# Retention's heads overlapped and stick-breaking cut to 512 queries, with its dense groups reordered

## What is computed

```python
proj = hn @ w_in
rq, rk, rv, rg, sq, sk, sv, ga, gb = split(proj)
q_r = rotary(heads(rq, 4)) * 256 ** -0.5        # 4 heads of 256, values of 512
k_r = rotary(heads(rk, 4))
y_ret = head_groupnorm(retention(q_r, k_r, heads(rv, 4)))   # decay g_h ** (t - s), causal
y_ret = (silu(rg) * y_ret) @ w_ret_out
y_sb = stick_breaking(heads(sq, 16), heads(sk, 16), heads(sv, 16)) @ w_sb_out
merged = sigmoid(ga) * y_ret + sigmoid(gb) * y_sb
mix = merged @ w_out
```

## Time and profile before

| | us |
|---|---|
| median of 3 runs (3181.03 to 3189.07) | 3181.04 |
| the profiled execution | 3180.37 |
| its span in the trace | 3178.6 |
| TensorE busy over the span (94%) | 2988.1 |
| VectorE (DVE) busy (46%) | 1473.8 |
| ScalarE (ACT) busy (34%) | 1082.3 |

### The profile page before, as it was taken

One profiled execution on the slowest core, in us unless ns is written; L12 is line 12 of the kernel. 1 busy time (PEld: TensorE's weight loads), 2 busy tenths in 40 slices (PEclk: granted clock), 3 DMA queues, 4 the chain that ended last, 5 costly groups with the idle time before them and its releaser, 6 DMA issues.

```text
span 3178.6 us, 47047 instructions
## 1 busy us (share of the span) xinstructions
PE 2988.1 (94%) x18149; PEld 2585.7 (81%) x18149; DVE 1473.8 (46%) x2073; ACT 1082.3 (34%) x1706; POOL 203.3 (6%) x169
## 2 busy tenths in 40 slices
PE   8999999999999766999999898998999999899997
PEld 7887789999999666899987786776888887678885
DVE  5554445553344666555543443344433334544423
ACT  4334333332333333343322222132334443333221
POOL 1000010000100232100001101001000000200000
PEclk9999999999999877999999999999999999899998
DMA  4221123233333000133333132131311112233331
GB/s 120 57 60 50 50 60 92 86 91 86 118 93 86 26 0 0 53 93 92 91 89 108 53 93 62 57 95 34 96 51 40 48 45 63 70 93 93 91 97 57
DMA packets 419421, 225.50 MB, mean 71 GB/s; under 512 B 7461, under 2 KB 416294, under 8 KB 419222
## 3 DMA queue, kind: packets, MB, share of 16 engines
q1 hardware_dynamic: 416310, 211.45, 23.2%
q0 software_dynamic: 2256, 10.32, 1.0%
q10 hardware_dynamic: 784, 2.75, 0.2%
HBM read 222.36 MB, written 2.13 MB: 71 GB/s over the span
## 4 chain that ended last, share of the span: by engine, by line
PE 83%; issue 10%; DVE 4%; ACT 2%; POOL 1%; DMA 0%; DVEq 0%; POOLq 0%; ACTq 0%
PE ps L425 36%; PE ps L421 28%; PE ps L630 3%; PE ps L712 2%; PE ps L804 2%; PE ps L914 2%; PE ps L900 1%; PE ps L714 1%; PE ps L871 1%; PE ps L724 1%; PE ps L634 1%; PE ps L817 1%; PE ps L903 1%; PE ps L695 1%; DVE g_qk L1700 0%
## 5 line engine op out<-in xcount | busy, mean ns | idle before, releaser
L393 DVE TENSOR_TENSOR wl<-raw,wh 128x1024 fp32r<-128x1024 f32 (+2 forms) x421 | 511.6, 1215 | 430.7 <-ACT wh L389 428.7
L389 ACT ACTIVATE wh<-raw 128x1024 fp32r<-128x1024 f32 (+2 forms) x421 | 425.8, 1011 | 802.2 <-PE ps L421 426.4
L425 PE MATMUL ps<-xh,wh 128*128 128x264 f32 x2736 | 565.2, 288 | 7.8 <-DVE xl L454 6.0
L425 PE MATMUL ps<-xl,wh 128*128 128x264 f32 x2736 | 559.0, 286 | 0.0
L425 PE MATMUL ps<-xh,wl 128*128 128x264 f32 x2736 | 558.5, 286 | 0.0
L425 PEld LDWEIGHTS ps<-xh,wh 128*128 128x128 f32 x2736 | 428.6, 189 | 14.5 <-issue 3.9
L425 PEld LDWEIGHTS ps<-xl,wh 128*128 128x128 f32 x2736 | 426.0, 189 | 0.0
L425 PEld LDWEIGHTS ps<-xh,wl 128*128 128x128 f32 x2736 | 425.2, 189 | 0.0
L421 PE MATMUL ps<-xh,wh 128*128 128x512 f32 x976 | 393.6, 403 | 17.9 <-DVE xl L454 14.0
L421 PE MATMUL ps<-xl,wh 128*128 128x512 f32 x976 | 389.0, 399 | 0.0
L421 PE MATMUL ps<-xh,wl 128*128 128x512 f32 x976 | 386.8, 396 | 0.0
(11 more groups left out here) (292 smaller groups left out, 4051.2 us busy)
## 6 DMA issues: line engine op xcount, KB each, us to landing
raw<-in_w_in SPq DMA_DIRECT2D x88, 512.0 KB, 4.0
raw<-in_ffn_w_gate SPq DMA_DIRECT2D x44, 512.0 KB, 3.8
raw<-in_ffn_w_up SPq DMA_DIRECT2D x44, 512.0 KB, 3.8
raw<-in_w_ffn_in SPq DMA_DIRECT2D x44, 512.0 KB, 3.8
raw<-in_fox_w_in SPq DMA_DIRECT2D x33, 512.0 KB, 4.1
raw<-in_hgrn_w_in SPq DMA_DIRECT2D x32, 512.0 KB, 4.0
raw<-in_ffn_w_down SPq DMA_DIRECT2D x32, 448.0 KB, 3.7
raw<-in_ffn_w_down SPq DMA_DIRECT2D x16, 512.0 KB, 3.9
```

Of the source, the lines that this page charges most:

```text
L389: nc.scalar.activation(wh[:, v % 2, 0:nk, :], raw[:, v % RAW_SLOTS, 0:nk, :], ACT.Copy).then_inc(s("w_hi"), 1)
L393: nc.vector.tensor_tensor(wl[:, v % 2, 0:nk, :], raw[:, v % RAW_SLOTS, 0:nk, :], wh[:, v % 2, 0:nk, :].bitcast(F32), ALU.subtract).then_in ...
L425: last = nc.tensor.matmul(ps[:, bank + b, 0:HALF], w[:, slot, kk, :], x[:, k, b * HALF:(b + 1) * HALF], start=first, stop=end_)
```

## The change

**Retention.** The heads are pipelined. A prologue `PH_RETP` makes q0, q1, k0, k1, v0, v1 of head 0 and its scores and decay. A pass of `PH_RET` (three) then makes `RET_REST` of its own head (v2, v3, g0 to g3), `RET_NEXT` of the next (q0, q1, k0, k1, v0, v1) and its own output projection; the last head (`PH_RETL`) makes the five `ga` groups where the others have `RET_NEXT`. Groups are as many in sum, and as many narrow and wide. TensorE's pass (where lines are left out stand the transposes and the values' matmuls, unchanged):

```diff
+            for gj in range(3):
+                group(gj)
+            pe.wait_ge(s("psum_free"), evacuated(PH_RETL, 0, 1) if last_ else evacuated(PH_RET, i, 1))
             pe.wait_ge(s("r_s_ready"), i + 2)
...
+            last.then_inc(s("r_vt_mm"), 1)
+            group(3)
+            pe.wait_ge(s("r_vt_ready"), 2 * i + 1)
...
+            group(4)
             pe.wait_ge(s("r_vt_ready"), 2 * i + 2)
...
+            group(5)
+            group(6)
             mean(0, "r_mu_mm")
+            group(7)
+            group(8)
             mean(1, "r_var_mm")
+            for gj in range(9, n_out):
+                group(gj)
             for m in range(KT):
+                group(n_out + m, ("r_out_ready", 4 * i) if m == 0 else None)
+                if m == 3 and not last_:
+                    ret_scores(i + 1)
```

On DVE the order of a pass becomes:

```diff
+            for uj in range(7):
+                split(uj)
+                take(uj)
             dve.wait_ge(s("r_mu_mm"), i + 1)
...
+            split(7)
+            take(7)
+            if not last:
+                dve.wait_ge(s("psum_free"), evacuated(ph, n, 7))
+                rotate(i + 1, 0)
+            split(8)
+            take(8)
             dve.wait_ge(s("r_r"), i + 1)
+            dve.wait_ge(s("r_g"), 4 * i + 4)
...
+                if e == 1:
+                    split(9)
+                    take(9)
+            split(10)
...
+            take(10)
+            if not last:
+                dve.wait_ge(s("psum_free"), evacuated(ph, n, 9))
+                rotate(i + 1, 1)
+                split(11)
+                take(11)
...
+                if m == 4 and not last:
+                    decayed(i + 1)
```

**Stick-breaking, 512 queries.** The strips become retention's (`QSTRIP`, 512, 400, 272, 144 and 16 columns), for the real tokens only:

```diff
-            for j in (0, 1, 3, 2):
-                nc.tensor.matmul(flat[:, STRIP0[j]:STRIP0[j] + SEQ - P * j], s_k[lo:hi, P * j:P * j + P],
-                                 s_q[lo:hi, P * j:SEQ], start=(j != 3), stop=False, skip_group_check=True)
             for j in range(NTT):
-                nc.tensor.matmul(flat[:, tail_at(j):tail_at(j) + TAIL], s_k[lo:hi, P * j:P * j + P],
-                                 s_q[lo:hi, SEQ:L], start=False, stop=False, skip_group_check=True)
+                nc.tensor.matmul(flat[:, QSTRIP[j]:QSTRIP[j] + SEQ - QFIRST[j]], s_k[lo:hi, P * j:P * j + P],
+                                 s_q[lo:hi, QFIRST[j]:SEQ], start=(j < 3), stop=False, skip_group_check=True)
```

**Stick-breaking, order.** The groups become values, gate, queries, keys; the transposes of the values (`sb_turn`) move from ahead of the sums to behind the last group:

```diff
+            ahead_(0)
             if not isinstance(i, int) or i:
                 sb_values(i - 1, 1)
+            sb_sums(2 * i)
+            ahead_(1)
+            pe.wait_ge(s("sb_a"), 2 * i + 1)
+            sb_z(1)
+            ahead_(2)
+            pe.wait_ge(s("sb_vt_ready"), i + 1)
+            pe.wait_ge(s("sb_o_done"), i + 1)
+            sb_values(i, 0)
+            sb_sums(2 * i + 1)
+            ahead_(3)
+            if not last:
+                pe.wait_ge(s("psum_free"), evacuated(PH_SB, i, 0))
+                sb_turn()
+                pe.wait_ge(s("psum_free"), evacuated(PH_SB, i, 3))
+                pe.wait_ge(s("sb_a"), 2 * i + 2)
+                sb_z(0)
```

More of the change, by code:

```diff
@@ L276, in program @@
     a = Area(after_yr, end)
+    b = Area(norms_at, arena)
+    ident_r, later_r, tri_r, one_r = (b.take(f"{n}_r", [P, P], F32R) for n in ("ident", "later", "tri", "one"))
+    assert b.at <= norms_at + 4 * L
     gb = a.take("gb", [P, KT, L])
@@ L840, in _, with ret_scores @@
         feed_forward(1, PH_UP1, PH_DOWN1, 3, 3)
[L843 to L857, removed]
+        def ret_scores(i):
             pe.wait_ge(s("r_rot"), i + 1)
@@ L1230, in _, with ret, high @@
         residual(PH_DOWN1, 4, ROW_MIXPRE)
-        def ret(i, norm=None):
+        for uj in range(N_NEXT):
+            split_ahead(act, act_hi, PH_RETP, 0, uj)
+            if uj == 0:
+                act_rstd(act, 4)
+        def ret(i, last=False):
+            ph, n = (PH_RETL, 0) if last else (PH_RET, i)
             def split(uj):
-                split_ahead(act, act_hi, PH_RET, i, uj)
+                split_ahead(act, act_hi, ph, n, uj)
             def gate(uj):
-                act.wait_ge(s("psum_free"), evacuated(PH_RET, i, uj))
-                nc.scalar.activation(rt[:, uj, META:L], rt[:, uj, META:L], ACT.Silu).then_inc(s("r_g"), 1)
-            for uj in range(8):
-                split(uj)
-                if norm and uj == 0:
-                    norm()
+                act.wait_ge(s("psum_free"), evacuated(ph, n, uj))
+                t = rt[:, RET_ROW["g"] + uj - 2, META:L]
+                nc.scalar.activation(t, t, ACT.Silu).then_inc(s("r_g"), 1)
+            def high(e):
+                act.wait_ge(s("r_out"), 4 * i + e + 1)
+                copy(rh[:, e, META:L], r_y[:, e, :]).then_inc(s("r_out_hi"), 1)
+            tables_for(act, "silu")
+            split(0)
+            split(1)
+            split(2)
+            gate(2)
             act.wait_ge(s("r_vt_mm"), 2 * i + 1)
             copy(r_vt[:, 0:NFULL, :], ps[:, 4:8, :]).then_inc(s("r_vt_ready"), 1)
+            split(3)
+            gate(3)
             act.wait_ge(s("r_vt_mm"), 2 * i + 2)
             copy(r_vt[0:TAIL, NFULL, :], ps[0:TAIL, 7, :]).then_inc(s("r_vt_ready"), 1)
-            split(8)
+            split(4)
+            gate(4)
+            split(5)
             act.wait_ge(s("r_y_mm"), i + 1)
             copy(r_y[:, :, :], ps[:, 4:8, :]).then_inc(s("r_y_ready"), 1)
-            split(9)
-            gate(8)
+            split(6)
+            gate(5)
+            tables_for(act, "ln_exp")
+            split(7)
             for e in range(4):
```

313 lines of the change are left out of this document (165 added, 148 removed).

## The result

| | before | after |
|---|---|---|
| median of the runs, us | 3181.03 (3179.16 to 3189.07, 4 runs) | 3085.14 (3083.71 to 3086.73, 4 runs) |
| profiled execution, us | 3180.37 | 3086.73 |
| its span, us | 3178.6 | 3085.0 |

The ratio is 0.9694, interval [0.9676, 0.9712]: faster by 95.9 us, to 3085.14 us where 3091 (3077 to 3114) was predicted.

The account below looks back on a forecast made before the run. TensorE was taken to bound both stages, by gaps in retention, matmul count and price in stick-breaking, and half clock. 59.8 + 17.9 - 3.5 + 15.7 = 89.9 us off 3180.37 gave 3091 us, range 3077 to 3114.

Parts of the forecast that it names:

- Retention: 59.8 us predicted: Retention stage: 45.5 us of TensorE waits and 19.6 us of half clock go, less 5.3 us coming back.
- what was to come back (5.3 us): Retention: 3.3 us of new TensorE waits on DVE, plus 2 us for more changes between dense groups and small matmuls.
- just in time: Retention, DVE: take 7, first rotation and split 8 end at 12.2 us, as group 8 ends; no wait.
- Stick-breaking, work: Stick-breaking matmuls: cheaper `z` and values, sums slightly dearer, sixteen times; 17.9 us saved, bounds 12 and 20.
- Order: 3.5 us predicted: Stick-breaking: keys come last, so the next pair's `z` waits for their eviction; 0.5 us seven times lost, bounds 2.5 and 7.
- Clock: 15.7 us predicted: Stick-breaking: half-clock stretches follow `z` with its tails; 3 of 18.7 us stay, 15.7 go, bounds 0 and 18.7.
- The dense groups on both sides of `z(1)`: Stick-breaking: with these and the tails gone, `z(1)` was expected to lower the clock no more.
- The first, that the half clock stays: Stick-breaking rival: stretches occur without idle time, so removing idle time can't cure them; 3107 us, chance 0.20.
- seven drops: Stick-breaking: if transposes don't count as busy, a drop of 1.7 us stays at each `z(0)`; 3100 us in all.
- The second rival: Retention: DVE becomes the bound of groups 9 to 11, 5 us a head; 3111 us, chance 0.12.
- The third: Retention rival: the chain still ends bare at the output projection, 6.67 + 2.4 us a head return; 3127 us, chance 0.04.
- the slower one: Retention rival: the whole chain lies bare on DVE, 39 us a head at most; 3247 us, chance 0.02.

Follow-up runs that it names:

- e8: Changed kernel with three thrown-away DVE multiplies added ahead of each head's first rotation; 3103.2 us in its one run.
- e4: Changed kernel with DVE's split 11, for out tile 0, put ahead of the second rotation; 3081.52 us, ratio 0.9688.
- e9: Kernel before with only the 512 queries in stick-breaking, nothing else changed; 3144.89 us, ratio 0.9884.
- e2: Changed kernel with the old stick-breaking order of groups (values, queries, keys, gate) and transposes, 512 queries kept; 3081.02 us, ratio 0.9687.
- e3: Changed kernel with the new order kept but 528 queries and the 16-column tails put back; 3121.09 us, ratio 0.9812.
- e5: Changed kernel with five thrown-away 16-column matmuls added to each `z`; 3120.02 us, ratio 0.9792.
- e6: Changed kernel with three thrown-away matmuls of 256, 256 and 128 columns added to each `z`; 3105.88 us, ratio 0.9748.
- e10: The changed kernel itself, unaltered, measured again in a second study; 3087.79 us, ratio 0.9705.
- e1: Changed kernel with all of stick-breaking put back (528 queries, strips, order), retention kept; 3125.69 us, ratio 0.982.
- e7: Changed kernel with old stick-breaking order, split 11 ahead of the second rotation, decay multiplies one output tile later, last head's ACT split ahead of the fifth sigmoid; 3073.84 us.

## Why the prediction was right

**Retention: 59.8 us predicted, 64.1 measured.** All 45.5 us of waits and all the half clock went, as the text had it: nothing but the stretch at the entry of the stage is left. Of what was to come back (5.3 us), the listed waits on `wl` come to 3.3 us, the sum that was forecast, but their places are not those of the forecast, and the agreement of the sum is luck. The timeline of DVE in head 1:

```profile
1939.82 0.69 DVE L1517 TENSOR_TENSOR rt<-ps,rstd 128x512 f32<-128x512 f32 x1 [0.99 <-PE ps L425]
...
1945.06 1.22 DVE L397 TENSOR_TENSOR wl<-raw,wh 128x1024 fp32r<-128x1024 f32 x1
...
1959.30 0.70 DVE L1517 TENSOR_TENSOR rt<-ps,rstd 128x528 f32<-128x528 f32 x1
1963.99 0.69 DVE L397 TENSOR_TENSOR wl<-raw,wh 128x512 fp32r<-128x512 f32 x1 [0.15 <-DVE rt L1802]
...
1984.79 1.73 DVE L1811 TENSOR_TENSOR r_s<-ps,decay 128x512 f32<-128x512 f32 x4
```

- The first rotation stands between take 7 and split 8, which ends at 1946.28; group 9, which needs it, began at 1946.33. The forecast put this split "just in time", with no cost, and 0.2 us on split 9, which cost nothing (it ended at 1951.90, ahead of group 9's end). In fact TensorE did wait for split 8: group 9 starts 0.86 us behind the variance, where behind the mean, and behind both in the last head, which has no rotation, it is 0.46. That is 0.40 us in each of three heads, 1.2 us, which no listing shows, since the modelled end of the variance covers it. e8 confirms it: all of the 3.75 us more came through.
- Behind the second rotation the split of the first half group (split 11) came at 1963.99, and TensorE waited 0.63 us, forecast 0.7. e4 took this wait away.
- A third, of 0.24 us at output tile 6, was not foreseen: the decay multiplies of the next head (1984.79) stand ahead of that split on DVE. The last head waited 0.65 us, not 0.4.
- The 4.3 us by which the step was short: idle time fell by 43.6 us, which is 45.5 and the 1.3 us of waits on `r_sum` that the forecast left out, less 3.3. The 2 us set aside for more changes between dense groups and small matmuls don't show as such. Busy time fell by 20.5 us, where 19.6 was worked out and 19.1 is half of what was busy at half clock; the other 1.4 us can't be put to one place, but the waits that went cost more than their listed idle time (below).

**Stick-breaking, work: 17.9 us predicted.** From e9, stage minus half its time at half clock: 377.3 - 18.7 = 358.6 against 340.8, so 17.8 us. `z` was forecast at 2.57 (2.55), the values at 2.53 (2.59), the sums at +0.08 (+0.1).

**Order: 3.5 us predicted, 4.4 measured** (e4 against e2). The 0.33 us listed as idle ahead of `z(0)` would make 2.3 us in seven loops; the forecast's 0.5 with the drain was nearer. From start to start it is 1.04 us for the transposes with the wait less 0.46 for the transposes alone, 0.58 a loop, 4.1 of the 4.4 us. The covers held: no wait on `s_sh` stands in any listing.

**Clock: 15.7 us predicted, 18.7 less 1.5 = 17 measured.** Its size was forecast, and half of its cause held: the prediction put the stretches down to the tails of `z` "run into half-width values". e2, e3, e5 and e6 confirm the tails. The values have no part that shows: eight of the nine stretches of before began ahead of the first matmul of the values and the ninth 0.07 us into them, all within 4.1 us of the start of a `z`. The first one, at 2313.1, by the timeline of before:

```profile
2309.44 2.42 PE L900 MATMUL ps<-lnt,s_k 64*128 64x512 f32 x8
2311.70 1.18 PE L903 MATMUL ps<-lnt,s_k 64*128 64x16 f32 x10
2312.82 1.04 PE L907 MATMUL ps<-later_r,ident_r 128*128 128x128 f32 x5
2313.78 3.69 PE L630 MATMUL ps<-s_a,s_vt 128*64 128x512 f32 x8
```

The dense groups on both sides of `z(1)`, which were to help, neither help nor are needed: e5 has them, and the clock fell at 2345.1 us in the masks of a `z(1)`, ahead of the group behind it; in e2 and e9 the neighbours of before stand, without half clock. That the forecast didn't rest on them alone is its luck. The prediction kept 3 us for the wait ahead of `z(0)`; one stretch of 3.4 us did follow a `z(0)` (at 2313.2 us in after, at 2444.7 in e10, none in e4).

The sum was 89.9 us against 93.6 on the profiled execution. Term by term the time differs from the forecast by -4.3 (retention), +0.9 (order), -1.3 (clock) and +1 us ahead of and behind the two stages.

**The rivals.** The first, that the half clock stays, fell: it argued that the stretches come without idle time and so can't be cured by removing it. The premise is right, and e9, e5 and e6 show it, but the change's cure was another: the tails. Two rules of the Trainium skill (TensorE: Matmul & The Clock Gate) were weighed. There the Trainium skill says (Part 4: PE-mode transpose) that transposes don't count as TensorE being busy as matmuls do; by it the prediction expected seven drops, one ahead of every `z(0)`, if it decided here. The trace has 1 in 7, and e4 with the same transposes and waits none. There the Trainium skill also says (A second HAM failure mode: psum-queue depth-cycling) that short idle times between groups make the clock swing; seven of 0.25 to 0.33 us in e4 left it at full, so this kernel's trace doesn't bear that out at this length. In e8 the clock fell at two of four waits of 3.6 to 3.9 us.

The second rival, DVE as the bound of groups 9 to 11, was closer than its chance of 0.12 says: DVE is the bound of group 9 and of the first half group in every looping head, with no margin left by e8. It cost 0.4 and 0.9 us a head and not 5; that its marks came no later was luck, since nothing was left between them and TensorE. The third and the slower one found no support: no wait on `rl` is left.

## What to carry to other kernels

Before removing idle time to win the clock back, find the stretches at half clock that have no idle time, and look what TensorE runs there: here five matmuls of 16 columns in each `z` cost 1.1 us as work and as much again in clock. Time each part of a change by itself: the reordering, which was to help the clock, brought none and cost 4.4 us. On an engine that works off its jobs in program order, put what the bounding engine waits for (the split) ahead of the long job that nobody is waiting for (the rotation). To see a wait that the listing misses, compare start to next start at two like places.

## What was not expected of the hardware

- The clock falls with TensorE busy throughout when 16-column matmuls are in the mix (e5, 38 us at half clock) and stays up when 128- to 256-column ones fill the same time (e6, none).
- The same stick-breaking code lost 18.7 us to half clock in the traced execution of before and 29 us in that of e1, where only the work ahead of it had changed; and the one stretch of after and of e10, the same kernel, lies in different pairs. A single part's gain isn't exactly what it is beside other parts. What sets where the stretches fall, the work ahead or the single execution, remains open.
- A wait costs more than its listed idle time, which is counted from the modelled end of the last matmul: 2.7 us for 1.9 in e4, 5.0 for 3.3 in e7, 4.4 for 2.3 in the seven loops of the order. Set start by start against e7, the waits of 0.63 us in after cost 0.9 us, those of 0.24 us 0.5 us, and 0.40 us went at the variance with nothing listed.
- The part of the kernel ahead of both stages, which no edit touches, differed by up to 5 us between profiles (the norm's sum at 1727.1 to 1732.0 us), so differences of a few microseconds were read from the stages, not from the totals.
